# Seven weight operands per pair: summed once on VectorE in three even passes and stored, or summed by GpSimd in every pass

## The reference

```python
xn = rmsnorm(x, norm_w)
q, k, v, i_pre, f_pre, o_pre, z_m, b_g, c_g, x_c, z_c, g_m, g_c = split(xn @ w_in)
h, C1, n1, m1 = mlstm_chunkwise(q, k * DQK ** -0.5, v, ig, lf, C0, n0, m0)
h = headnorm(h) * head_norm_w * sigmoid(o_pre) * silu(z_m);  y_m = h @ w_proj_m
cv, conv1 = short_conv(c_g * x_c, conv0, conv_w)
y_c = (silu(z_c) * b_g * cv) @ w_proj_c
mix = sigmoid(g_m) * y_m + sigmoid(g_c) * y_c
out = x + mix @ w_out;  y = rmsnorm(out, final_norm_w)
```

## Time and profile before

| | us |
|---|---|
| median of 3 runs | 2635.06 (2633.59 to 2636.96) |
| profiled execution | 2633.47 |
| its span | 2631.5 |
| phase B's first to last product | 234.5 to 2050.2 |
| PE, DVE, ACT, POOL busy | 2390.0, 1734.1, 885.8, 812.6 |

### The profile page before, as it was taken

One profiled execution on the slowest core, in us unless ns is written; L12 is line 12 of the kernel. 1 busy time (PEld: TensorE's weight loads), 2 busy tenths in 40 slices (PEclk: granted clock), 3 DMA queues, 4 the chain that ended last, 5 costly groups with the idle time before them and its releaser, 6 DMA issues. The chain is left out here.

```text
span 2631.5 us, 43480 instructions
## 1 busy us (share of the span) xinstructions
PE 2390.0 (91%) x14697; PEld 2304.4 (88%) x14697; DVE 1734.1 (66%) x2556; ACT 885.8 (34%) x1613; POOL 812.6 (31%) x558
## 2 busy tenths in 40 slices
PE   7996986898868997999998898999999899999998
PEld 7995986897767897998998897998999899999886
DVE  4334796788888886678889676777898533234333
ACT  4322443443333333443333443444333310001111
POOL 0003543444345443434535443343344000000000
PEclk9997998998978998999999998999999999999999
DMA  5343445642334544553432434555333645334542
GB/s 184 126 132 99 118 116 128 161 122 73 93 114 130 171 135 128 160 158 91 121 97 67 127 95 116 140 147 138 86 89 85 215 129 160 101 102 132 154 138 88
DMA packets 428812, 326.74 MB, mean 124 GB/s; under 512 B 25786, under 2 KB 396602, under 8 KB 428726
## 3 DMA queue, kind: packets, MB, share of 16 engines
q1 hardware_dynamic: 428726, 325.62, 44.1%
HBM read 236.51 MB, written 89.10 MB: 124 GB/s over the span
## 5 line engine op out<-in xcount | busy, mean ns | idle before, releaser
L1435 PE MATMUL b_g<-x_hi,w_hi 128*128 128x384 f32 (+1 forms) x3024 | 1005.3, 332 | 113.2 <-DVE part L1128 67.4
L1435 PE MATMUL b_g<-x_lo,w_hi 128*128 128x384 f32 (+1 forms) x3024 | 980.2, 324 | 0.0
L1435 PE MATMUL b_g<-x_hi,w_lo 128*128 128x384 f32 (+1 forms) x3024 | 979.7, 324 | 0.0
L1435 PEld LDWEIGHTS b_g<-x_hi,w_hi 128*128 128x128 f32 x3024 | 591.5, 196 | 128.5 <-DVE part L1128 46.7
L1435 PEld LDWEIGHTS b_g<-x_lo,w_hi 128*128 128x128 f32 x3024 | 591.8, 196 | 2.1
L1435 PEld LDWEIGHTS b_g<-x_hi,w_lo 128*128 128x128 f32 x3024 | 589.6, 195 | 0.0
L1110 DVE TENSOR_TENSOR w_lo<-stages,w_hi 128x512 fp32r<-128x512 f32 x270 | 263.5, 976 | 62.9 <-ACT w_hi L988 58.2
L1110 DVE TENSOR_TENSOR w_lo<-w_raw,w_hi 128x512 fp32r<-128x512 f32 x270 | 242.1, 897 | 83.5 <-ACT w_hi L988 78.7
L1758 PE MATMUL c_g<-act_hi,RH 128*128 128x294 f32 x896 | 268.2, 299 | 11.5 <-DVE act_lo L1708 11.5
L1758 PE MATMUL c_g<-act_hi,RL 128*128 128x294 f32 x896 | 268.1, 299 | 0.0
L1758 PE MATMUL c_g<-act_lo,RH 128*128 128x294 f32 x896 | 267.6, 299 | 0.0
(11 more groups left out here) (251 smaller groups left out, 3484.5 us busy)
## 6 DMA issues: line engine op xcount, KB each, us to landing
stages<-w_in SPq DMA_DIRECT2D x108, 512.0 KB, 5.7
w_raw<-w_in SPq DMA_DIRECT2D x108, 512.0 KB, 5.2
act_stage<-cv_d SPq DMA_DIRECT2D x7, 1176.0 KB, 12.5
tanh_gate<-tm_d SPq DMA_DIRECT2D x7, 1176.0 KB, 5.9
tanh_gate<-tc_d SPq DMA_DIRECT2D x7, 1176.0 KB, 8.9
mix_d<-mix SPq DMA_DIRECT2D x7, 1176.0 KB, 6.9
xt<-x_prompt SPq DMA_DIRECT2D x16, 512.0 KB, 4.5
xT_d<-xT_raw SPq DMA_DIRECT2D x16, 512.0 KB, 4.7
```

The lines of the kernel that those rows point to most:

```text
L1435: last = nc.tensor.matmul(bank[:, 0:n], w[:, j, k, :], x[:, j, k, 0:n], start=(j < 4 and k == 0 and m == 0), stop=(k == 3 and m == 2), ski ...
```

## The change

- The passes are even: n = 344, 344, 340 instead of 260, 384, 384. The chunks are 5, 5 and 6.
- In pass 0 the raw blocks are loaded into the places of four of the seven operands. DVE makes the four sums two pairs ahead, one at each of steps 3 to 6. SP stores the seven operands as one block of 1.84 MB in w_ops_d. In passes 1 and 2 that block is loaded instead of the raw ones. POOL has no weight sums, but for pair 0, whose sums and split, and the first x split, are in phase A.
- The low part of operand j - 1 is subtracted at step j (that of operand 6 at the next pair's step 0).
- All four x quarters of the next pass are loaded at once, in the second conv body (load_quarters, "quarters" in SEGMENTS), with five places instead of four; the first x sums are one body before the turn.
- The first chunk's q, k, m and v are loaded at the head of the fourth oz body, the gate as before (in pass 1, q and k after the last sample's state has gone out).
- From POOL to DVE: the multiply of q (at step 2, ahead of the scores) and the decode's products of v and k. The norm of h becomes a scaled identity, and h is turned by a matmul with it.
- ACT's exponentials come before its step 0. The gate scans of pass 0 are spread over more steps. SP's program has no loops.

```diff
-PASSES = [(0, 260), (512, 384), (1280, 384)]
-TQ = 384
+PASSES = [(0, 344), (680, 344), (1368, 340)]
+TQ = 344
 NPP = 36
+NOP = 7
...
+        g.w_ops_d = dram("w_ops_d", NPP, P, NOP * 4 * P)
...
+        head = g.S[:, :, :].rearrange("p a n -> p (a n)")[:, 0:4 * 4 * P].rearrange("p (j k n) -> p j k n", j=4, k=4)
+        g.W7 = [(sbuf(nc, early, "w_operands0", [P, NOP, 4, P]),), (head, sbuf(nc, early, "w_operands1", [P, NOP - 4, 4, P]))]
...
+def load_blocks(eng, g, par, c0, c1, signal):
+
+    w = g.w_in[0].rearrange("(k p) n -> p k n", p=P)
+    for j, k0, c in ((0, 0, c0), (4, 4, c0), (2, 0, c1), (5, 4, c1)):
+        eng.dma_start(operand(g, par, j), w[:, k0:k0 + 4, bass.ds(c, P)]).then_inc(signal, 16)
...
+            load_blocks(sp, g, 0, COL["q"], COL["k"], w0_in)
...
+            pool.wait_ge(w0_in, 64)
+            w = g.W7[0][0]
+            nc.gpsimd.tensor_tensor(w[:, 3], w[:, 2], w[:, 5], ALU.add).then_inc(s_set, 1)
+            pool.wait_ge(s_set, 1)
+            nc.gpsimd.tensor_tensor(w[:, 1], w[:, 3], w[:, 0], ALU.subtract).then_inc(s_set, 1)
+            nc.gpsimd.tensor_tensor(w[:, 2], w[:, 0], w[:, 2], ALU.subtract).then_inc(s_set, 1)
+            pool.wait_ge(s_set, 2)
+            nc.gpsimd.tensor_tensor(w[:, 6], w[:, 4], w[:, 1], ALU.subtract).then_inc(s_set, 1)
...
+            act.wait_ge(s_set, 4)
+            for j in range(NOP):
+                nc.scalar.activation(g.LH[:, j], g.W7[0][0][:, j], ACT.Copy).then_inc(hi_set, 1)
+            act.wait_ge(xs_in, 64)
+            nc.scalar.activation(g.X0H[:, :, 0:PASSES[0][1]], quarter(g, 0, 0), ACT.Copy).then_inc(hi_set, 1)
...
-    CH0 = (0, 4, 10)
-    CHUNKS = (4, 6, 6)
+    CH0 = (0, 5, 10)
+    CHUNKS = (5, 5, 6)
...
+                if p == 0:
+                    half = half_of(p, s, i, q)
+                    sp.wait_ge(w_ops_out[q], (16, 32)[q] * half)
+                    load_blocks(sp, g, q, *columns(s, i, q), w_raw_in[q])
+                else:
+                    if isinstance(pair, int) and pair < NPP + 2:
+                        sp.wait_ge(w_ops_out[q], (16, 32)[q] * (NPP // 2))
+                    at = FIRST[s] + 2 * i + q
+                    src = g.w_ops_d[at] if isinstance(at, int) else g.w_ops_d[bass.ds(at, 1)].rearrange("a p n -> (a p) n")
+                    for n, part in enumerate(g.W7[q]):
+                        flat = part[:, :, :, :].rearrange("p j k n -> p (j k n)")
+                        sp.dma_start(flat, src[:, 2048 * n:2048 * n + flat.shape[1]]).then_inc(w_ops_in[q], 16)
...
+            def store_w(pair, par):
+
+                sp.wait_ge(s_set, 4 * pair + 4)
+                dst = g.w_ops_d[pair] if isinstance(pair, int) else g.w_ops_d[bass.ds(pair, 1)].rearrange("a p n -> (a p) n")
+                for n, part in enumerate(g.W7[par]):
+                    flat = part[:, :, :, :].rearrange("p j k n -> p (j k n)")
+                    sp.dma_start(dst[:, 2048 * n:2048 * n + flat.shape[1]], flat).then_inc(w_ops_out[par], 16)
...
-                for slot, k0, at in ((0, 0, c0), (1, 0, c0 + n), (2, 4, c0 + n)):
+                for slot, k0, at in ((0, 0, c0), (1, 0, c0 + n), (2, 4, c0 + n), (4, 4, c0)):
...
+                if p == 0:
+                    store_w(pair + 1, 1)
+                if s == "oz" and isinstance(i, int) and i == 3:
+                    for par in range(2):
+                        sp.wait_ge(row_out[p][par], 1 + 16 * DMAS[p] * (2 * ROWS["qk"][par] + 3 * ROWS["oz"][par]))
+                    if p == 0:
+                        sp.wait_ge(misc_out, 48)
+                    if p != 1:
+                        load_kq(CH0[p])
+                    load_m(CH0[p])
+                    load_v(CH0[p])
...
                     load_w(pair + 3, *following, 1)
+                    if following[0] == 0:
+                        store_w(pair + 2, 0)
...
-            def sums(pair, half, par):
-
-                for blk in range(2):
-                    pool.wait_ge(w_in_s[par][blk], 16 * (half + 1))
-                w = RW[par]
-                pool.wait_ge(w_ready, 7 * pair + 4)
-                nc.gpsimd.tensor_tensor(SB[:, 0], w[:, 1, 0:4, :], w[:, 1, 4:8, :], ALU.add).then_inc(s_set, 1)
-                nc.gpsimd.tensor_tensor(w[:, 1, 0:4, :], w[:, 0, 0:4, :], w[:, 1, 0:4, :], ALU.subtract).then_inc(s_set, 1)
-                pool.wait_ge(s_set, 4 * pair + 2)
-                nc.gpsimd.tensor_tensor(SB[:, 1], SB[:, 0], w[:, 0, 0:4, :], ALU.subtract).then_inc(s_set, 1)
-
-            def last_sum(pair, par):
-
-                w = RW[par]
-                pool.wait_ge(w_ready, 7 * pair + 7 + 5)
-                pool.wait_ge(s_set, 4 * pair + 3)
-                nc.gpsimd.tensor_tensor(w[:, 0, 4:8, :], w[:, 0, 4:8, :], SB[:, 1], ALU.subtract).then_inc(s_set, 1)
...
-            def chunk_query(c):
-                pool.wait_ge(kq_in, 32 * (c + 1))
-                pool.wait_ge(wint_set, c + 1)
-                nc.gpsimd.tensor_tensor(QW[:, :, :], QW[:, :, :], qT[:, :, :], ALU.mult).then_inc(qw_set, 1)
-
-            def chunk_norm(c):
...
-                pool.wait_ge(rs_set, c + 1)
-                nc.gpsimd.tensor_tensor(HB[:, :, :], HB[:, :, :], bc(ss[:, 2, :], DHV), ALU.mult).then_inc(hn_set, 1)
...
+            def sums(pair, half, par, at):
+
+                w = [operand(g, par, j) for j in range(NOP)]
+                if at == 0:
+                    dve.wait_ge(w_raw_in[par], 64 * (half + (1 if par else 0)))
+                    nc.vector.tensor_tensor(w[3], w[2], w[5], ALU.add).then_inc(s_set, 1)
+                elif at == 1:
+                    dve.wait_ge(s_set, 4 * pair + 1)
+                    nc.vector.tensor_tensor(w[1], w[3], w[0], ALU.subtract).then_inc(s_set, 1)
+                elif at == 2:
+                    nc.vector.tensor_tensor(w[2], w[0], w[2], ALU.subtract).then_inc(s_set, 1)
+                else:
+                    dve.wait_ge(s_set, 4 * pair + 2)
+                    nc.vector.tensor_tensor(w[6], w[4], w[1], ALU.subtract).then_inc(s_set, 1)
...
+                if j == 0:
+                    if not first_pair(p, s, i, q):
+                        w_low(NOP - 1, pair, q)
+                elif not final_pair(p, s, i, q):
+                    w_low(j - 1, pair + 1, 1 - q)
...
+                    dve.wait_ge(kq_in, 32 * (c + 1))
+                    dve.wait_ge(wint_set, c + 1)
+                    nc.vector.tensor_tensor(QW[:, :, :], QW[:, :, :], qT[:, :, :], ALU.mult).then_inc(qw_set, 1)
...
+                elif at == 12:
+                    dve.wait_ge(rs_set, c + 1)
+                    for h in range(NH):
+                        last = nc.vector.tensor_scalar(Dm[:, h, :], g.ident[:, :], ss[:, 2, h:h + 1], None, ALU.mult)
+                    last.then_inc(hn_set, 1)
...
+                    vb = dec[:, 5, sl(b, KB)].rearrange("p (h a) -> p h a", a=2)
+                    for a in range(2):
+                        last = nc.vector.tensor_tensor(HB[:, :, a * P:(a + 1) * P], kT[:, :, :], bc(vb[:, :, a], P), ALU.mult)
+                    link(last)
...
+                        if p == 0 and extra != "turn" and j >= 3:
+                            sums(pair_of(p, s, i, q) + 2, half_of(p, s, i, q) + 1, q, j - 3)
+                        if extra == "turn" and q == 1 and j:
+                            x_low(p + 1, j - 1)
...
-                        last = nc.tensor.transpose(PT[k // 4][:, k % 4, :], HB[:, k // 2, (k % 2) * P:(k % 2 + 1) * P], g.ident[:, :])
+                        last = nc.tensor.matmul(PT[k // 4][:, k % 4, :], HB[:, k // 2, (k % 2) * P:(k % 2 + 1) * P], Dm[:, k // 2, :],
+                                                start=True, stop=True)
```

298 lines of the change are left out of this document (125 added, 173 removed).

## The result

The changed kernel takes 2537.35 us (median of 4 runs, 2534.89 to 2539.08) against 2635.23 for the kernel before: a ratio of 0.9628, 95% interval 0.9611 to 0.9644. Forecast were 2453 us, with a range of 2395 to 2535. The profiled execution took 2534.89 us against 2633.47 before, so the gain is 98.6 us where the sum had 182. The sign was right, the size was little over half of what was forecast, and the time is 2.4 us above the range.

The account below looks back on a forecast made before the run. TensorE was taken as the bound on average, with some 409 of 1816 us excess, mostly late qT loads and late VectorE. Terms of 46+36+27+14+42+17=182 us off 2633.5 gave 2451.5, forecast 2453, range 2395 to 2535.

Parts of the forecast that it names:

- What bounds the kernel: Whole kernel: TensorE bound on average; some 409 of 1816 us are excess, mostly from late qT loads and late VectorE.
- Pass 0 outside chunks and turn: Pass 0's other pairs: longer pairs cover VectorE's work, raw block waits leave 26 of 53 us, 27 us less.
- Start: Pairs 0 to 3 of pass 0: excess 14 instead of 30, 2 us given back, so 14 us less.
- passes 1 and 2 elsewhere: Remaining pairs of passes 1 and 2: ready-made block loads stay covered, change 0 us.
- Chunks: 16 chunks: TensorE's waits vanish, leaving 139 us against 174.5, 36 us less; bounds +35 and -13.
- the waits were TensorE's own: Rival, chance 0.12: chunk waits stay because the multiply sits in front of the scores, +36 us, kernel at 2490 us.
- The h term: In each chunk, turning h by matmuls instead of transposes takes 1.78 us, +1.0 us each, +16 us over 16 chunks.
- The wait for qT: Single pairs before the chunks: earlier loads leave 5 of 51 us, 46 us less; bounds 0 and 12 left.
- Turns and decode: Pass changes: early x quarters, 42 us less; decode in pass 1: GpSimd's products moved to VectorE, 17 us less.
- Columns: TensorE's product matmuls in all passes: even column counts cost 0 us; upper bound 21 us more.
- VectorE keeps pass 0: Rival, chance 0.16: with the sums on VectorE, raw blocks come late in 17 bodies of pass 0, +59 us, 2510 us.
- The DMA queue decides: Rival, chance 0.06: the queue gives only 150 GB/s in pass 0, +380 us, kernel slower at 2830 us.

Follow-up runs that it names:

- late sums: The changed kernel with VectorE's four weight sums of pass 0 two products later, so raw blocks have 3.8 us more to land: 2513.71 us.
- early sums: The changed kernel without the stored block, raw loads and VectorE's four sums in all three passes, sums at their unmoved place: 2622.31 us.
- the two runs with late sums: VectorE's sums two products later, on the changed kernel (2513.71 us) and on the changed kernel without the stored block (2547.88 us).
- seven small edits: Changed kernel: chunk multiplies, mask and decode loads earlier, h by transposes, two decode C buffers, turn differences on VectorE, pass 0 sums two products later: 2435.60 us.
- the seventh: Pass 0's sums two products later, added to the changed kernel with the six other edits together (2471.42 us): 2435.60 us.
- the best one: The changed kernel with all seven small edits together: 2435.60 us, ratio 0.9246 to the kernel before.

## Why the prediction was half right

*What bounds the kernel.* Right in the main. Nearly half of the loss was in pass 0, leaving out GpSimd's sums gave 124 us, 84 of them there, and the low parts fell to 0.71 us as told. But that they cost by contention is not shown: the sums also came late for ScalarE, and with GpSimd making them two pairs ahead in the changed kernel they cost little beside what their order costs: nothing in the even chunk pairs, and 3.9 and 3.0 us over pairs 4 to 10 and 22 to 31 against VectorE's late sums (92.3 and 136.3 us). One reading was loose: the 0.41 us of the earlier trace rows was no row beside a GpSimd sum, since the sum before it had ended at 612.40; what it was read for holds all the same (see the last section).

*Pass 0 outside chunks and turn.* Right in size (26.9 us against 26) and in mechanism: "The new wait is that of the sums for the raw block", and giving the block more time took 10.7 us of it in pairs 4 to 10 and 11.7 in pairs 22 to 31.

*Start, passes 1 and 2 elsewhere.* Right within some 1 us each (17.2 us against 16, 3.2 against 4.3). In the start two terms were off and cancel: the excess is 17.2 and not 14, and the end of phase A is 0.2 us later and not 2. "Passes 1 and 2 elsewhere: 0" was right as a difference and left out what the stored block is worth: without it and with the early sums these two passes lasted 67 and 28 us longer.

*Chunks.* This is the step that failed: "The rest of today's 10.1 us per chunk (60.3/6) is waiting ... I take that wait as gone". Three things are wrong in it. The window's average is not the steady chunk: in the kernel before a steady one of pass 2 is 9.2 us (5.51 and 3.64 beyond its two pairs), and the first and the late conv chunks lift the mean to 10.1. TensorE's own work was put too low, at 7.9 us where 8.5 are measured. And the wait for the scores did not go: it comes from VectorE's order, behind the evacuation of product 1, and moving the two multiplies ahead of it removed it, where the faster low parts had not. The rival "the waits were TensorE's own", at 0.12 and +36 us, came about for the chunks. Its reason, the multiply in front of the scores, can be part of it (0.68 us of work ahead of a wait of 0.84); but the wait was there before the change without that multiply (1.41 us), and no run moves the multiply by itself. A steady chunk of pass 2 now takes 9.6 us: 8.5 of TensorE's own work and 1.1 of wait. Against 7.9 that is 27 us over 16 chunks; the 17.7 us of the first chunk pairs come on top; and of the 13 us set aside for queues and the second conv chunk 8 were needed. With 179.8 us the chunks are the only term outside its own bounds (139 + 35 = 174). The h term held: 1.81 us measured for 1.78, 2.3 times the transposes. The Trainium skill ("TensorE: Matmul & The Clock Gate", Terms) has 4 times for transpose mode in FP32, which this trace does not bear out; the sum was right to go by the row.

*The wait for qT.* "Of 51 us I leave 5": the wait for qT is gone in full. Of the 8.7 us left in the windows some 4 are the chunk's opening matmuls and 4 are a late raw block in pass 0 (pair 11 falls from 18.5 to 14.4 us with the late sums). But 17.7 us came up in the first chunk pairs, where the mask stands behind the finish of the oz row, and the forecast has no term for what comes late next. The early issue is worth 25 us.

*Turns and decode.* 59 us left against 36. Turns and "dec_first" have 29 us against 17. 9.3 of these are in the pair with the decode's first loads, late on SP, for which the forecast gives no figure of its own; issuing them earlier gave 6.9. Each turn's two GpSimd differences held VectorE, which gave 3.7 us when taken away, the least certain of these gains. The decode window has 30 us against 19. The round trip of the C state was sized well (19.9 us of excess in its four pairs against 4 x 4, where its own 17.6 less 13.1 makes 4.5 each; two buffers gave 13.2), and most of the rest is pair 0, the first after the turn, at 7.3 us, which the decode's sum has no term for.

*Columns.* "A line through both gives 0.1557 at 344" from 260 and 384 columns; the pitch is 0.1569 at 344 and 0.1563 at 340 columns, so 0.1 and 0.2 us per pair and 14.6 us in all. The bound was 21; the line was 0.8% too low at 344 columns and 1.6% at 340. Why stays open: the kernel before with even passes has other pitches at the same columns (13.26 and 13.06 us a pair).

*The other rivals.* VectorE keeps pass 0: not to the extent of 59 us. Lateness behind the raw block was real, 23.7 us, and is the mechanism that the forecast itself counted; the load of 27.4 us of work against 26.2 was not what held the conv pairs. The DMA queue decides: no. Pass 0 moved 190 to 300 GB/s, and in the run with late sums one pair ran at a share of 1.00 and 347 GB/s with TensorE busy throughout. The 150 GB/s of the earlier trace rows was what was asked, not what the queue could give. The stores cost some 10 us of pass 0, by the two runs with late sums.

*The range.* The four misses, chunks without their first pairs, the wait for qT with them, turns with decode, and columns, have one sign (+23, +21, +23, +15 us). Every term but the chunks stayed within its own bounds; the range stops well short of all upper bounds together. The first three have this in common, that a term was costed without what stands behind it in an engine's order. The fourth has not, and that it fell on the same side is chance as far as is known.

## What to carry to other kernels

Engines work in order, so a late operand is first a question of order: look for an engine that sits idle behind one wait while the operation that another engine needs is queued behind it. Here seven small edits, four of them nothing but such moves, gave as much as the whole change. Gains measured one by one need not add: here six overlapped by 11 us and the seventh gave 12 more in company than alone. When a stall is taken away, read from the trace what the next operation of the same chain waits for, and cost a steady stretch from a steady stretch, not from the mean of a window with an odd end.

## What the runs showed of the hardware

**A long wait of TensorE cost more than its length.** TensorE in a decode pair of the changed kernel, and the window of its restart (the column after POOL is the granted clock):

```profile
891.26 0.53 PE L1453 MATMUL b_g<-x_hi,w_hi 128*128 128x344 f32 x1 [4.75 <-DVE rows L1132]
891.59 0.49 PE L1453 MATMUL b_g<-x_lo,w_hi 128*128 128x344 f32 x1
...
895.12 0.32 PE L1453 MATMUL b_g<-x_hi,w_lo 128*128 128x344 f32 x1
```

```profile
891.20:894.80 3.60, 3.54 (x13) 3.54 (x14) 3.44 (x6) 0.00 (x0) 0.00 (x0) 0.53 0.60 255
```

After 4.75 us idle the next twelve matmuls start 0.29 us apart instead of 0.157, at the lower of the two clocks (granted 0.53, 1.2 GHz), which adds 1.6 us to the hole. The forecast counted waits at their length. The mean clock rose from 0.977 in the changed kernel to 0.987 in the best one; how much of the gains is this part was not separated.

**A GpSimd operation held VectorE's subtraction for its whole length, not for a share.** VectorE in the second turn of the changed kernel, and GpSimd beside it:

```profile
1392.98 3.43 DVE L1095 TENSOR_TENSOR w_lo<-w_operands,w_hi 128x512 fp32r<-128x512 f32 x1
...
1399.20 3.38 DVE L1095 TENSOR_TENSOR w_lo<-w_operands,w_hi 128x512 fp32r<-128x512 f32 x1
```

```profile
1392.71 3.13 POOL L920 TENSOR_TENSOR x_quarters<-x_quarters 128x1360 f32<-128x1360 f32 x1 [32.12 <-DVE x_lo L1116]
1398.94 3.10 POOL L926 TENSOR_TENSOR x_quarters<-x_quarters 128x1360 f32<-128x1360 f32 x1 [3.09 <-DVE x_lo L1116]
```

Each low part started 0.3 us behind a difference and ended some 0.6 us after it; the first took 3.43 us instead of 0.69. Not every operation of VectorE is held so: in the kernel before, an evacuation of PSUM with 260 columns took 0.43 us (642.67 to 643.09) wholly inside a sum of GpSimd (642.54 to 643.82). The forecast named this rule of the Trainium skill ("SBUF — State Buffer", Who interferes with whom) and left it inside a bound; the trace agrees with it. How much of a turn's remaining excess is VectorE's work and how much the lower clock was not separated, and stays open.
